# Spreading a row by stacked rounded products, and moving weight splits between VectorE's products

## The chip, the cores and the metric

The kernel runs on one core of one Trainium2 chip. The metric is the device time of one execution in microseconds; the time before is the median of three runs, 1167.11 us (1166.09 to 1169.34).

## What is computed

The model is two blocks over 256 tokens of width 1024. The change touches two mixers of the second block. The first is a linear attention with four heads, in which a running maximum over the tokens weighs each score:

```
dmat = where(tri, bcum[t] - bcum[s] + i[s], -inf)
m_t  = maximum(inter, max(dmat))
s    = einsum('td,sd->ts', q, k) * exp(dmat - m_t)
den  = w_inter * q.n + sum(s)
h    = num / maximum(abs(den), exp(-m_t))
```

The second is an eight-head softmax attention over the 256 tokens, the last attention of the model:

```
q = rope(rmsnorm(q)) ; k = rope(rmsnorm(k))
o[h] = softmax(mask(q[h] @ k[h].T) / sqrt(128)) @ v[h]
out = concat(o) @ w_o
```

Around them stand three feed-forward stages (up projection, a convolution of width 3, gate, down projection). All operands are fp32.

## The kernel before

**Weights.** All projections read one stream of weights, cut into slots of 128 x 1024 elements. SyncE loads a slot into a ring of eight, as TensorE gives slots back. TensorE multiplies in the rounded fp32 type, so each operand is split in two: ScalarE writes the rounded upper half of the slot (its split), then VectorE writes the rest in place (`split_one`, a subtraction over 128 x 1024, L1863). A projection then takes three rounded products for each block. TensorE waits for VectorE's half before the first block of each slot. ScalarE may write the upper half of a slot only when TensorE has begun the slot three earlier, since those halves have a ring of four.

**Order.** Each engine runs one list of instructions in program order. The places of the splits in VectorE's list are written out by hand, as `split_to(n)`: do all splits up to slot n. Any instruction of VectorE that stands ahead of a split delays it, and any split that stands ahead of a product delays the product.

**Linear heads.** VectorE forms rows of four partitions, one per head: a scan for the cumulated gates (`rowF`), the row `rowG`, a scan for the running maximum, and its sum with `rowF`. The last two fill `rowM2` (L2372 and L2373). Behind them stand the splits of slots 161 to 164 and 165 (`split_to(L0+4)`, L0 is 164). TensorE meanwhile runs the value projections lv (slots 156 to 163) and lo0 (164, 165). It then takes the heads one by one (`l_scores`, L1080): the product `mb` spreads a head's row over 128 partitions, by a 4 x 128 matrix of ones and zeros (`sel`) times the 4 x 512 row, in plain fp32; `sc` is the head's score product. VectorE adds the mask (`decay_in`), ScalarE takes the exponential, VectorE multiplies by the scores (`weighted`), TensorE makes the sum and the values (`l_values`: `dn`, `nm`) and the norm's sum (`hn`). Between them TensorE runs halves of the projections lo1 to lo3 (`gate_half`).

**Last attention.** TensorE projects bq, bk, bv. VectorE rotates q and k (`rope`), then multiplies each by its heads' inverse norms (`head_scaled`, four products over 128 x 512, for q and for k). On bk's and bv's slots the order of VectorE's list is: splits up to slot 263, q's four products, splits of 264 to 266, k's rotation (with 267 and 268 inside), k's four products, splits of 269 to 271. The slots 262 to 269 are bv's, 270 and later are those of the output projection bo. TensorE makes scores 0 and 1 ahead of the last two k-steps of bv10 and bv11 (slot 269); scores 2 need a bank that ScalarE frees by copying bv10. Then the heads turn in a ring: `a_max` (VectorE: mask and row extreme), `a_exp` (ScalarE: exponential with its sum), the scaling by the inverse sum (VectorE, L2534 to L2537), `turn` (TensorE: three transposes, L1168), a copy (ScalarE), `values` (TensorE), copies of the result (ScalarE), and the rest of its split (GpSimd). VectorE's order is a_max 0, a_max 1, scaling 0, a_max 2, scaling 1, a_max 3, scaling 2 and so on.

Of the kernel before, what the change touches and what calls it, by code (L numbers as in the profile page):

```python
# [21 lines left out]
ALU = mybir.AluOpType  # L22
# [3 lines left out]
P = 128  # L26
T = 256
# [41 lines left out]
def constants():  # L69

    c = np.zeros((P, NCON), np.float32)

    def put(name, a):
        at, k = CCOL[name]
        c[:a.shape[0], at:at + k] = a
    i = np.arange(P)
    s, t = i[:, None], i[None, :]
    same = (s // CH) == (t // CH)
    put("ident", np.eye(P))
    put("ones", np.ones((P, P)))  # L80
    put("bones", same * 1.0)
    strict, incl = same & (s < t), same & (s <= t)
    put("mask4", np.concatenate([strict * 1.0, incl * 1.0, strict * -1.0, incl * 1.0], 1))
    lev = []
    for m in (1, 2, 4, 8, 16, 32):

        off = (s // (2 * m) == t // (2 * m)) & ((s // m) % 2 == 1) & ((t // m) % 2 == 0)
        level = np.eye(P) - off
        lev.append(np.concatenate([level[:CH, :CH], level[CH:, CH:]], 0))
    put("lev", np.concatenate(lev, 1))  # L90
    put("idc", (s % CH == np.arange(CH)[None, :]) * 1.0)
    put("rev", (s >= t) * 1.0)
    z = np.zeros((P, P))
    put("negS", np.concatenate([(s >= t) * NEG, z, (s >= t) * NEG], 1))
    put("posI", np.concatenate([(s > t) * -NEG, z], 1))
    put("negC", np.concatenate([(t > s) * NEG, z, (t > s) * NEG], 1))
    half = 16
    inv = 500000.0 ** (-np.arange(0, 32, 2, dtype=np.float32) / np.float32(32))
    ang = np.arange(T, dtype=np.float32)[None, :] * inv.astype(np.float32)[:, None]
    cos, sin = np.ones((P, T)), np.zeros((P, T))  # L100
    cos[:half] = cos[half:2 * half] = np.cos(ang)
    sin[:half], sin[half:2 * half] = np.sin(ang), -np.sin(ang)
    put("cos", cos)
    put("sin", sin)
    put("scan", np.tile((np.arange(T) % CH != 0) * 1.0, (P, 1)))
    sel = np.zeros((4, 4 * P))
    for h in range(4):
        sel[h, h * P:(h + 1) * P] = 1.0
    put("sel", sel)
    put("one", np.ones((P, T)))  # L110
    put("eps", np.tile(np.array([[1e-6, 64e-5]]), (P, 1)))
    return c
# [32 lines left out]
SLOT_END = slot_ends()  # L145
# [35 lines left out]
def program(nc, ins, out):  # L181
    ctx = ExitStack()
    with ctx:
        sems = {}

        def sem(name):
            if name not in sems:
                sems[name] = ctx.enter_context(nc.semaphore(name))
            return sems[name]
# [55 lines left out]
        def view(kb, c, n, off=0):  # L245
            at = int(kb * KB) + off
            half = int(MID * KB)
            assert at >= half or at + c * n <= half
            v = arena[:, at:at + c * n] if at < half else arena2[:, at - half:at - half + c * n]
            return v.rearrange("p (c n) -> p c n", c=c) if c > 1 else v  # L250
# [11 lines left out]
        base = 78.5  # L262
# [76 lines left out]
        rowF = view(base + 25, 1, T)  # L339
        rowG = view(base + 26, 1, T)  # L340
        rowM2 = view(base + 27, 1, 2 * T)
        rowT = view(base + 29, 1, T)
        EM = view(base + 30, 2, T)
        ET = view(base + 32, 2, 384)
# [7 lines left out]
        ak = view(base + 8, KD, T)  # L352
        aq = view(base + 16, KD, T)
# [13 lines left out]
        def cst(name, rows=P):  # L367
            at, k = CCOL[name]
            if at >= NCON1:
                return con2[0:rows, at - NCON1:at - NCON1 + k]  # L370
            return con1[0:rows, at:at + k]
# [12 lines left out]
        def fr(ap):  # L384

            first = ap.tensor.name == arena.name
            row = int(MID * KB) if first else int((ARENA - MID) * KB)
            part_, at = ap.offset // row, ap.offset % row + (0 if first else int(MID * KB))
            for (a, b), place in zip(places, rounded):
                if a * KB <= at < b * KB:  # L390
                    w = int((b - a) * KB)
                    return bass.AP(tensor=place, offset=part_ * w + at - int(a * KB),
                                   ap=[[w, ap.ap[0][1]]] + [list(x) for x in ap.ap[1:]])
            raise AssertionError(at / KB)
# [12 lines left out]
        def rd(ap):  # L407

            return fr(ap).bitcast(F32)
# [68 lines left out]
        def _(pe):  # L478
            state = {"slot": 0, "blk": 0, "A": 0, "B": 0, "C": 0, "inc": False}

            def mm(o, l, r, start, stop, shared=False):
                ins_ = nc.tensor.matmul(o, l, r, start=start, stop=stop, skip_group_check=shared)  # L482
                if state["inc"]:
                    ins_.then_inc(sem("slots_used"), 1)
                    state["inc"] = False
                return ins_
# [38 lines left out]
            def close(ins_, name):  # L525
                ins_.then_inc(full(name)[0], 1)
# [226 lines left out]
            for u, name in enumerate(("mqn0", "mqn1", "mkn0", "mkn1")):  # L753
                o = open_(name)
# [95 lines left out]
            for i in range(0, 16, 2):  # L850
                t, c = i // 8, i % 8 // 2
                o = [open_(f"qd{i}"), open_(f"qd{i + 1}")]
# [227 lines left out]
            def l_scores(h):  # L1080
                o = open_(f"mb{h}")
                if h == 0:
                    ready(pe, "m_row")
                close(mm(o[:, :], cst("sel", 4)[:, h * P:(h + 1) * P], rowM2[0:4, :], True, True), f"mb{h}")
                o = open_(f"sc{h}")
                if h == 0:
                    pe.wait_ge(*freed("lk1"))
                mm(o[:, 0:T], lqk[:, 4 + h, 0:P], lqk[:, h, :], True, True)
                close(mm(o[:, T:T + P], lqk[:, 4 + h, P:T], lqk[:, h, P:T], True, True), f"sc{h}")
# [757 lines left out]
        def _(dve):  # L1847
            own = [0]

            def mark(ins_):  # L1850
                own[0] += 1
                ins_.then_inc(sem("dve_step"), 1)
# [4 lines left out]
            def step(ins_):  # L1857

                mark(ins_)
                settle()  # L1860
# [7 lines left out]
            def split_to(end):  # L1868
                while split[0] < min(end, nslots):
                    split_one(split[0], split[0] + 1)  # L1870
                    split[0] += 1
# [17 lines left out]
            def tt(o, a, b, op):  # L1889
                return V.tensor_tensor(o, a, b, op)  # L1890
# [451 lines left out]
            ffn(0, "r2", "n2", "x2", "l", "an")  # L2342

            dve.wait_ge(sem("ld_con"), 48)
            split_to(SLOT_END["lq0"] + 3)
            dve.wait_ge(*freed("r3"))
            step(V.reciprocal(rstd, rstd))
# [21 lines left out]
            step(V.tensor_tensor_scan(rowF[0:4, :], cst("one", 4), rowLF[0:4, :], 0.0, ALU.mult, ALU.add))  # L2369
            tt(rowG[0:4, :], rowG[0:4, :], rowF[0:4, :], ALU.subtract).then_inc(sem("g_row"), 1)  # L2370
            ready(dve, "g_row")
            step(V.tensor_tensor_scan(rowM2[0:4, 0:T], cst("one", 4), rowG[0:4, :], 0.0, ALU.mult, ALU.max))  # L2372
            tt(rowM2[0:4, T:2 * T], rowM2[0:4, 0:T], rowF[0:4, :], ALU.add).then_inc(sem("m_row"), 1)  # L2373

            def decay_in(h):
                o = take(f"mb{h}")
# [121 lines left out]
                    if u % 2:  # L2498
                        split_to(min(split[0] + 1, end))

            def head_scaled(x, dst, n0):

                settle()
                for u in range(4):
                    c = slice(2 * u, 2 * u + 2)
                    ready(dve, "a_inv", n0 + u + 1)
                    tt(dst[:, c, :], atm[x][:, c, :], asq[x][:, c, :], ALU.mult).then_inc(sem("a_rope"), 1)
            split_to(SLOT_END["bk1"] + 2)
            rope("q", aq, 0, SLOT_END["bk2"] + 2)
            split_to(SLOT_END["bk3"] + 2)  # L2510
            head_scaled("q", aq, 0)
            split_to(SLOT_END["bk3"] + 5)
            rope("k", ak, 4, SLOT_END["bk3"] + 7)
            head_scaled("k", ak, 4)
            split_to(SLOT_END["bv11"] + 2)

            def a_max(h):
                o = take(f"as{h}")
                if h >= 3:
                    dve.wait_ge(*full(f"at{h - 3}"))  # L2520
                for t in range(TT):
                    s = slice(t * P, 3 * P if t else P)
                    last = V.tensor_tensor_reduce(aP[:, h % 3, s], o[:, s], cst("negC")[:, s], -P ** -0.5, 3e38,  # L2523
                                                  ALU.add, ALU.min, small[:, 56 + 2 * h + t:57 + 2 * h + t])
                    if t == 0:
                        mark(last)
                    else:
                        release(last, f"as{h}")
            a_max(0)
            a_max(1)  # L2530
            for h in range(8):
                ready(dve, "a_e", 2 * h + 2)
                rs = small[:, 72 + 2 * h:74 + 2 * h]
                step(V.reciprocal(rs, rs))  # L2534
                p_ = aP[:, h % 3, :]
                step(V.tensor_scalar(p_[:, 0:P], p_[:, 0:P], rs[:, 0:1], None, ALU.mult))
                V.tensor_scalar(p_[:, P:3 * P], p_[:, P:3 * P], rs[:, 1:2], None, ALU.mult)\  # L2537
                    .then_inc(sem("a_p"), 1)
                if h < 6:
                    a_max(h + 2)  # L2540
            split_to(SLOT_END["bv11"] + 3)
# [90 lines left out]
```

## Time and profile before

| | value |
|---|---|
| median of three runs | 1167.11 us |
| the profiled execution | 1166.16 us, of which the span is 1164.4 us |
| TensorE busy | 1141.5 us, 98% of the span |
| VectorE busy | 936.8 us, 80% |
| ScalarE busy | 694.9 us, 60% |
| granted TensorE clock | 1.0 of full speed (2.4 GHz) throughout |

The page's chain of work is followed back from the last instruction. A piece of it that belongs to TensorE is time that only shorter or fewer products save; a piece of VectorE or ScalarE is time in which TensorE had to wait for them. Times in the timelines are microseconds from the span's start.

### The profile page before, as it was taken

The page shows a single profiled execution, that of the slowest core. Times are in us where ns is not written, and L with a number is a line of the kernel's source. Part 1 is how long each engine was busy: PE and PEld are TensorE (multiplying, and loading weights), DVE is VectorE, ACT ScalarE, POOL GpSimd, SP SyncE. Part 2 cuts the span into 40 slices and gives each one's busy share as a digit, 9 for nine tenths or more (in the row PEclk, how much of TensorE's full clock was granted, in tenths as well). Part 3 has the DMA queues.
Part 4 walks back from the last instruction along what each step waited for, and adds up shares of the span by engine and source line. Part 5 has one row for each costly group of instructions (what it writes and reads, how often), then busy time and mean ns, then how long its engine had stood idle before and what let it go on. Part 6 is the DMA issues. An engine that isn't in the chain of part 4 may idle for free.

```text
span 1164.4 us, 23202 instructions
## 1 busy us (share of the span) xinstructions
PE 1141.5 (98%) x9164; PEld 1052.7 (90%) x9164; DVE 936.8 (80%) x1369; ACT 694.9 (60%) x1075; POOL 332.0 (29%) x252
## 2 busy tenths in 40 slices
PE   9999999999999999999999999999999999999998
PEld 8988778878899999989888999998899789999987
DVE  5989774458878999866658799998679968999963
ACT  6787854346656666644557566665455666666642
POOL 2334111000013555311202235552128123555500
PEclk9999999999999999999999999999999999999999
DMA  8744211225556555554442455555554425555552
GB/s 311 238 151 140 97 37 40 86 98 199 188 189 203 184 186 186 176 189 176 157 156 93 151 192 182 182 182 182 196 178 155 145 86 181 181 183 182 181 186 86
DMA packets 55012, 188.95 MB, mean 162 GB/s; under 512 B 6144, under 2 KB 7296, under 8 KB 54784
## 3 DMA queue, kind: packets, MB, share of 16 engines
q1 hardware_dynamic: 53312, 182.48, 45.0%
q10 hardware_dynamic: 1600, 5.05, 1.3%
q8 instruction: 73, 1.20, 0.4%
q14 instruction: 27, 0.22, 0.1%
HBM read 186.46 MB, written 1.05 MB: 161 GB/s over the span
## 4 chain that ended last, share of the span: by engine, by line
PE 51%; DVE 36%; issue 6%; ACT 6%; DMA 1%; SPq 0%; ACTq 0%; DVEq 0%
PE psA L482 41%; DVE rounded L1890 18%; DVE arena L1893 13%; PE psB L482 9%; DVE arena L1890 3%; ACT rounded L1236 2%; ACT arena L1236 2%; ACT L1236 1%; DMA arena<-in_w 1%; DVE arena L2300 0%; DVE rounded L1893 0%; PE psB L792 0%; PE psB L1168 0%; DVE arena L2523 0%; PE psB L775 0%
## 5 line engine op out<-in xcount | busy, mean ns | idle before, releaser
L482 PE MATMUL psA<-rounded,rounded 128*128 128x256 f32 (+1 forms) x7236 | 1003.3, 300 | 11.0 <-DVE rounded L1890 10.0
L482 PEld LDWEIGHTS psA<-rounded,rounded 128*128 128x128 f32 x7236 | 940.0, 191 | 67.0 <-DVE rounded L1890 12.3
L1890 DVE TENSOR_TENSOR rounded<-arena,rounded 128x1024 fp32r<-128x1024 f32 (+2 forms) x364 | 475.5, 1338 | 61.3 <-ACT rounded L1236 58.7
L1236 ACT ACTIVATE rounded<-arena 128x1024 fp32r<-128x1024 f32 (+2 forms) x508 | 415.3, 858 | 168.8 <-DVE arena L2259 61.0
L1722 POOL TENSOR_TENSOR arena<-arena 128x256 f32<-128x256 f32 (+1 forms) x113 | 180.5, 1603 | 551.2 <-ACT arena L1236 201.1
L1236 ACT ACTIVATE arena<-arena 128x256 f32<-128x256 f32 (+8 forms) x313 | 163.3, 552 | 177.5 <-DVE arena L2324 109.4
L1893 DVE SCALAR_TENSOR_TENSOR arena<-arena 128x255 f32<-128x255 f32 (+4 forms) x338 | 190.6, 607 | 12.5 <-ACT arena L1236 9.9
L482 PE MATMUL psB<-arena 64*64 64x64 f32 (+9 forms) x1448 | 129.4, 281 | 4.4 <-issue 2.6
L482 PEld LDWEIGHTS psB<-arena 64*64 64x64 f32 (+4 forms) x1448 | 91.1, 152 | 31.5 <-issue 21.0
L1890 DVE TENSOR_TENSOR arena<-arena,psA 128x256 f32<-128x256 f32 (+1 forms) x101 | 45.5, 450 | 49.3 <-PE psA L482 39.0
L1807 POOL TENSOR_TENSOR rounded<-arena,rounded 128x256 fp32r<-128x256 f32 x63 | 71.9, 1142 | 34.0 <-ACT rounded L1236 34.0
L1236 ACT ACTIVATE arena<-psA 128x256 f32<-128x256 f32 (+2 forms) x75 | 35.3, 477 | 52.3 <-PE psA L482 51.7
L1890 DVE TENSOR_TENSOR arena<-arena 128x256 f32<-128x256 f32 (+5 forms) x85 | 55.2, 667 | 10.2 <-ACT arena L1236 8.7
L1890 DVE TENSOR_TENSOR arena<-psA,arena 128x512 f32<-128x512 f32 x79 | 54.0, 686 | 5.2 <-PE psA L482 2.4
L1236 ACT ACTIVATE arena<-psB 128x512 f32<-128x512 f32 (+4 forms) x61 | 28.4, 496 | 42.9 <-PE psB L482 40.1
L1236 ACT ACT_TABLE_LOAD x41 | 52.6, 1283 | 2.0 <-PEq L2626 1.2
L1890 DVE TENSOR_TENSOR arena<-psB,arena 128x512 f32<-128x512 f32 (+5 forms) x55 | 29.3, 561 | 28.6 <-PE psB L482 27.9
L1893 DVE SCALAR_TENSOR_TENSOR rounded<-arena,rounded 128x256 fp32r<-128x256 f32 x48 | 32.3, 687 | 18.2 <-ACT rounded L1236 18.2
L1728 POOL TENSOR_TENSOR rounded<-arena,rounded 128x256 fp32r<-128x256 f32 x24 | 21.7, 929 | 36.2 <-ACT rounded L1236 36.2
L1236 ACT ACTIVATE arena<-psB,arena 128x256 f32<-128x256 f32 (+1 forms) x45 | 23.6, 564 | 12.3 <-PE psB L482 7.1
L1737 POOL TENSOR_TENSOR arena<-arena 128x512 f32<-128x512 f32 x15 | 20.4, 1359 | 1.2
L1783 POOL TENSOR_TENSOR arena<-arena 64x256 f32<-64x256 f32 x8 | 5.9, 739 | 39.6 <-DVE arena L1890 39.3
(75 smaller groups left out, 183.7 us busy)
## 6 DMA issues: line engine op xcount, KB each, us to landing
arena<-in_w SPq DMA_DIRECT2D x343, 512.0 KB, 3.5
arena<-in_mem ACTq DMA_DIRECT2D x2, 512.0 KB, 7.3
arena<-in_x ACTq DMA_DIRECT2D x1, 1024.0 KB, 5.2
out<-arena SPq DMA_DIRECT2D x8, 128.0 KB, 3.3
arena<-in_con ACTq DMA_DIRECT2D x1, 992.0 KB, 5.9
arena<-in_con ACTq DMA_DIRECT2D x1, 960.0 KB, 7.4
arena<-in_w SPq DMA_DIRECT2D x2, 256.0 KB, 3.3
arena<-in_x SPq DMA_DIRECT2D x2, 256.0 KB, 5.0
```

The lines of the kernel that those rows point to most:

```text
L482: ins_ = nc.tensor.matmul(o, l, r, start=start, stop=stop, skip_group_check=shared)
L1236: return nc.scalar.activation(o, i, f, **kw)
L1722: return nc.gpsimd.tensor_tensor(o, a, b, ALU.mult)
L1728: nc.gpsimd.tensor_tensor(fr(x[:, c, :]), x[:, c, :], rd(upper_[:, c, :]), ALU.subtract)\
L1737: nc.gpsimd.tensor_tensor(dst[:, 0:2, :], dst[:, 0:2, :], dst[:, c, :], ALU.add)\
L1783: nc.gpsimd.tensor_tensor(LT[h, 4 * g:4 * g + 4, :], quadA[h, 4 * g:4 * g + 4, h], bc(cst("idc")[h], 4), ALU.add).then_inc(sem("LT"), 1)
L1807: nc.gpsimd.tensor_tensor(lr_, gv[:, j % 2, :], hi, ALU.subtract)\
L1890: return V.tensor_tensor(o, a, b, op)
L1893: return V.scalar_tensor_tensor(out=o, in0=a, scalar=s, in1=b, op0=op0, op1=op1)
```

## The change

It has two parts.

**The row's spread.** The constant `sel` gets 36 rows, with its four rows of ones a second time at 32 to 35, and VectorE rounds it once, ahead of the linear mixer's first splits. The scan and the sum now fill a plain row `rowM`. Its rounded upper part goes to partitions 0 to 3 of `rowM2` and the rest to 32 to 35; partitions 0 to 31 are set to zero first. The product `mb` is one of the rounded type over these 36 partitions. Per head it replaces the plain fp32 product over 4.

**The last attention.** In `head_scaled` a split follows the first and the third product. For q these are slots 264 and 265, with 266 behind the fourth product. For k they are 269 and 270; slot 271 is split after a_max 0 and a_max 1. VectorE's order at the heads becomes a_max 0, a_max 1, split 271, scaling 0, scaling 1, a_max 2, a_max 3, scaling 2, a_max 4, scaling 3, and so on.

```diff
-    sel = np.zeros((4, 4 * P))
+    sel = np.zeros((36, 4 * P))
     for h in range(4):
-        sel[h, h * P:(h + 1) * P] = 1.0
+        sel[h, h * P:(h + 1) * P] = sel[32 + h, h * P:(h + 1) * P] = 1.0
...
+        rowM = view(base + 58, 1, 2 * T)
...
-                close(mm(o[:, :], cst("sel", 4)[:, h * P:(h + 1) * P], rowM2[0:4, :], True, True), f"mb{h}")
+                close(mm(o[:, :], fr(cst("sel", 36))[:, h * P:(h + 1) * P], fr(rowM2)[0:36, :], True, True), f"mb{h}")
...
             dve.wait_ge(sem("ld_con"), 48)
+            mark(V.tensor_copy(fr(cst("sel", 36)), cst("sel", 36)))
             split_to(SLOT_END["lq0"] + 3)
...
-            step(V.tensor_tensor_scan(rowM2[0:4, 0:T], cst("one", 4), rowG[0:4, :], 0.0, ALU.mult, ALU.max))
-            tt(rowM2[0:4, T:2 * T], rowM2[0:4, 0:T], rowF[0:4, :], ALU.add).then_inc(sem("m_row"), 1)
+            mark(V.memset(rd(rowM2)[0:32, :], 0.0))
+            step(V.tensor_tensor_scan(rowM[0:4, 0:T], cst("one", 4), rowG[0:4, :], 0.0, ALU.mult, ALU.max))
+            step(tt(rowM[0:4, T:2 * T], rowM[0:4, 0:T], rowF[0:4, :], ALU.add))
+            step(V.tensor_copy(fr(rowM2)[0:4, :], rowM[0:4, :]))
+            tt(fr(rowM2)[32:36, :], rowM[0:4, :], rd(rowM2)[0:4, :], ALU.subtract).then_inc(sem("m_row"), 1)
...
-            def head_scaled(x, dst, n0):
+            def head_scaled(x, dst, n0, end):
...
                     tt(dst[:, c, :], atm[x][:, c, :], asq[x][:, c, :], ALU.mult).then_inc(sem("a_rope"), 1)
+                    if u % 2 == 0:
+                        split_to(min(split[0] + 1, end))
...
-            head_scaled("q", aq, 0)
+            head_scaled("q", aq, 0, SLOT_END["bk3"] + 5)
             split_to(SLOT_END["bk3"] + 5)
             rope("k", ak, 4, SLOT_END["bk3"] + 7)
-            head_scaled("k", ak, 4)
-            split_to(SLOT_END["bv11"] + 2)
+            head_scaled("k", ak, 4, SLOT_END["bv11"] + 1)
+            split_to(SLOT_END["bv11"] + 1)
...
             a_max(0)
             a_max(1)
-            for h in range(8):
+            split_to(SLOT_END["bv11"] + 2)
+            a_part(0)
+            a_part(1)
+            a_max(2)
+            a_max(3)
+            for h in range(2, 8):
+                a_part(h)
                 if h < 6:
                     a_max(h + 2)
```

`a_part(h)` holds the scaling of a head that stood in the loop's body before (L2534 to L2537).

## Rows read from the trace of the kernel before

**Rows 1.** The page, parts 1 and 4: busy time and the chain's shares.
```profile
PE 1141.5 (98%) x9164; PEld 1052.7 (90%) x9164; DVE 936.8 (80%) x1369; ACT 694.9 (60%) x1075; POOL 332.0 (29%) x252
...
PE 51%; DVE 36%; issue 6%; ACT 6%; DMA 1%; SPq 0%; ACTq 0%; DVEq 0%
```

**Rows 2.** Chain of work, 550 to 680: start us, us, what.
```profile
571.73 27.73 PE psA L482 x144
...
604.68 3.87 PE psB L482 x18
...
611.42 4.73 PE psB L482 x22
...
625.75 2.83 PE psB L482 x16
```

**Rows 3.** TensorE's groups by form, 571.6 to 594.6: count, busy us, mean ns.
```profile
L482 PE MATMUL psA<-rounded,rounded 128*128 128x512 f32 x96 | 22.1, 390 | 0.0
```

**Rows 4.** Timeline, 600 to 615: start us, us, engine, what, idle before and its releaser.
```profile
600.47 1.28 ACT L1236 ACT_TABLE_LOAD   x1
...
603.98 1.23 DVE L1890 TENSOR_TENSOR rounded<-arena,rounded 128x1024 fp32r<-128x1024 f32 x1 [2.23 <-ACT rounded L1236]
...
605.13 0.55 DVE L1890 TENSOR_TENSOR arena<-arena,psB 128x384 f32<-128x384 f32 x1
605.66 2.69 PEld L482 LDWEIGHTS psB<-arena 128*128 128x128 f32 x16 [0.76 <-issue]
...
612.50 0.75 DVE L1890 TENSOR_TENSOR arena<-psB,arena 128x256 f32<-128x256 f32 x2 [1.29 <-PE psB L482]
```

**Rows 5.** Timeline, 582 to 590: the row's end and what follows.
```profile
583.29 4.85 DVE L1890 TENSOR_TENSOR rounded<-arena,rounded 128x1024 fp32r<-128x1024 f32 x4
...
585.82 1.07 ACT L1236 ACTIVATE rounded<-arena 128x1024 fp32r<-128x1024 f32 x1 [0.45 <-PE psA L482]
```

**Rows 6.** VectorE's groups by form, whole span: count, busy us, mean ns, idle before.
```profile
L1890 DVE TENSOR_TENSOR rounded<-arena,rounded 128x512 fp32r<-128x512 f32 x9 | 6.0, 689 | 4.1 <-ACT rounded L1236 3.8
...
L2191 DVE COPY arena<-arena 64x512 f32<-64x512 f32 x1 | 0.4, 408 | 0.0
...
L1907 DVE MEMSET arena<- 128x256 f32 x1 | 0.3, 272 | 0.9 <-PEq L2626 0.9
```

**Rows 7.** Timeline, 549 to 552: VectorE ahead of the linear mixer.
```profile
549.87 1.22 DVE L1890 TENSOR_TENSOR rounded<-arena,rounded 128x1024 fp32r<-128x1024 f32 x1 [0.48 <-ACT rounded L1236]
```

**Rows 8.** Timeline, 904 to 924: q's products, the splits, k's products.
```profile
904.57 3.30 POOL L1722 TENSOR_TENSOR arena<-arena 128x512 f32<-128x512 f32 x2 [5.04 <-ACT arena L1236]
905.18 4.44 DVE L1890 TENSOR_TENSOR arena<-arena 128x512 f32<-128x512 f32 x4
909.54 3.48 DVE L1890 TENSOR_TENSOR rounded<-arena,rounded 128x1024 fp32r<-128x1024 f32 x3
...
910.81 5.76 PE L482 MATMUL psA<-rounded,rounded 128*128 128x512 f32 x24 [1.93 <-DVE rounded L1890]
...
923.72 2.50 DVE L1890 TENSOR_TENSOR arena<-arena 128x512 f32<-128x512 f32 x4 [0.91 <-ACT arena L1236]
```

**Rows 9.** Timeline, 929 to 948: the heads of the last attention.
```profile
929.54 0.28 DVE L2523 CUSTOM_DVE_ANT_0 arena<-psA,arena 128x128 f32<-128x128 f32 x1
...
932.63 0.92 PE L482 MATMUL psA<-arena 128*128 128x128 f32 x4 [0.38 <-ACT arena L1236]
...
933.59 0.29 DVE L2523 CUSTOM_DVE_ANT_0 arena<-psA,arena 128x128 f32<-128x128 f32 x1 [1.47 <-PE psA L482]
...
935.17 0.52 PE L1168 MATMUL psB<-arena 128*128 128x128 f32 x3 [0.63 <-DVE arena L2537]
...
940.00 0.39 ACT L1236 ACTIVATE arena<-arena 128x128 f32<-128x128 f32 x1
...
941.80 0.40 ACT L1236 ACTIVATE arena<-arena 128x128 f32<-128x128 f32 x1
...
943.88 0.39 ACT L1236 ACTIVATE arena<-arena 128x128 f32<-128x128 f32 x1
```

More of the change, by code:

```diff
@@ L2528, in a_max, with a_part @@
                         release(last, f"as{h}")
-            a_max(0)
-            a_max(1)
-            for h in range(8):
+            def a_part(h):
                 ready(dve, "a_e", 2 * h + 2)
@@ L2538, in _ @@
                     .then_inc(sem("a_p"), 1)
+            a_max(0)
+            a_max(1)
+            split_to(SLOT_END["bv11"] + 2)
[5 more added lines that the diff above has]
+                a_part(h)
                 if h < 6:
```

## The prediction, made before the changed kernel was seen

> **What bounds the kernel now.** I read the page first: TensorE is busy 98% of the span and holds 51% of the chain, VectorE 36% [rows 1]. An average says nothing of the two stages that change, so I read the chain of each, then its timeline.
>
> In the linear mixer the chain is TensorE alone from 571.73 us on, through all four heads. The reader is to see blocks of rounded projections, and between them one block per head on the other bank set [rows 2]. There a shorter product shortens the path, until another engine's result is late. The closest is VectorE's `weighted` 0 [rows 4].
>
> In the last attention three things take turns. TensorE stands 1.93 us before slot 264, until VectorE has split it [rows 8]. From 910.81 to 932.2 it is busy again. From 932.63 to 947.8 the heads go round, and all three engines are nearly full [rows 9].
>
> **Spread, what TensorE saves.** What a `mb` costs now comes out of the blocks of the chain. The block of 16 instructions (hn, dn, nm) has 3328 columns by instruction, each plain product being two: 2.83 us, or 0.85 ns a column [rows 2]. By that price sc, dn and nm of a head (768, 768 and 1536 columns) take 2.61 us, and the block of 18 leaves 3.87 - 2.61 = 1.26 us for `mb`; with hn (0.87) the block of 22 leaves 1.25. Its 1024 columns are worth 0.87 us; the other 0.4 us is a pause around a product of four rows, also seen as 0.76 us in which no weight load begins behind it [rows 4]. A rounded product of 512 columns costs 22.1 / 96 = 0.23 us [rows 3]. No row shows a product of 36 rows. From one side the pause goes (`mb` 0.23, 1.03 saved), from the other it grows by as much again (1.03, 0.23 saved). I take it as staying: 0.63, or 0.63 saved per head, since every row of a short product has it.
>
> The Trainium skill (TensorEngine Tiling (Array Packing), Key Properties) says that a change of tiling mode drains TensorE. The pause in the trace agrees with that, and 36 rows would still be a smaller tile than 128, so by it the drain stays, which speaks against the full gain. Read as a drain that goes with the small tile, the rule gives 0.63 a head; without it 1.03 would hold.
>
> **Spread, where the saving meets a wait.** The plain sum is 4 x 0.63 = 2.5 us. Head 0's sum `dn` also needs `weighted` 0, which ends at 605.13 + 0.55 = 605.68. That chain hangs on ScalarE's table load at 600.47, behind the small `gcol` product that stands ahead of `mb`, and on the split at 603.98, so it doesn't move [rows 4]. `dn` 0 begins now near 604.68 + 1.26 + 0.65 = 606.6, and cannot begin before 605.73. So after heads 0 and 1 the gain is 0.85, not 1.26. Heads 2 and 3 add 0.63 each: VectorE idles 1.29 us before `decay_in` 2 [rows 4], as much as it is then to come forward. Together 2.1 us, which pass on to hn 1 and so to the chain's next pieces in ScalarE and VectorE. Bounds: 0.23 a head gives 0.9; 1.03 a head gives 0.85 + 2 x 1.03 = 2.9.
>
> **Spread, what VectorE pays.** Four things are new ahead of the split of slot 161. The memset over 32 x 512 has 128 x 256 at 0.27 as nearest row, so 0.54 for twice the columns (0.27 to 0.69). The rounding copy of 4 x 512 has 64 x 512 at 0.41 (to 0.69). The subtraction has 128 x 512 at 0.69 [rows 6]. Two more waits for the own result take 0.1 or a little less. Sum 1.7 us, 1.4 to 2.2. Behind them in VectorE's list stand the splits of 161 to 165, and TensorE waits for those. Slot 161 is split by 583.29 + 1.21 = 584.50 now. TensorE begins it near 585.4: ScalarE was released at 585.80 by the end of its first product, which takes 0.39 [rows 3, 5]. So the margin is 0.9, and TensorE will stand 1.7 - 0.9 = 0.8 us (0.5 to 1.3). Slot 162 follows at 1.2 us in VectorE and 2.8 in TensorE, so nothing adds up. Rounding `sel` (0.4 to 0.7) comes ahead of the split at 549.87, before which VectorE idles 0.48 [rows 7]. It is taken at nothing; what is over the idle time, up to 0.2, would move this stage's later splits, and all 0.7 of it if that idle weren't there.
>
> Net for the spread: 2.1 - 0.8 = **1.3 us** (from 0.9 - 1.3 = -0.4 to 2.9 - 0.5 = 2.4).
>
> **Attention, q's side.** TensorE is at slot 264 at 908.88 and gets it at 910.81. After the change the split follows q's first product: 905.18 + 1.19 = 906.37, plus 1.2 to 1.9 for a split beside GpSimd, which works until 907.87. So it is there by 907.6 to 908.3, and the 1.93 us go [rows 8]. Slots 265 and 266 end at about 910.5 and 912.3 and are needed at 911.8 and 917.5. The products that move back have no hurry, as scores begin at 928. TensorE then has no gap until slot 269 is done, because from 910.81 on it had none.
>
> **Attention, k's side.** ScalarE's inverse norms follow TensorE's sums and come 1.2 us or more earlier, so k's products begin when VectorE is through with its rotation, about 0.9 earlier: it idled 0.91 there [rows 8]. VectorE's list from 905.18 to there is otherwise the same work. In it, slot 269 is ready long before 927.2; slot 270 must wait for ScalarE's upper half, which comes behind two copies at 925.3, in time for the split at 925.9. With one split fewer ahead, a_max 0 starts near 927.7 instead of 929.54 [rows 9]. Split 271 (1.16) then fills the time in which ScalarE takes the first exponentials; scaling 0 would follow near 930, with or without it. Scores 2 hang on the copy of bv10, that is on TensorE's last products (1.9 earlier) and on a_exp 1 (1.9 earlier): 930.75 instead of 932.63.
>
> **Attention, the ring.** Before, VectorE waited 1.47 us for scores 2 [rows 9] while scaling 1 was ready to go behind it; TensorE then stood 0.63 for scaling 1 at 935.17. Now scaling 1 fills that wait, turn 1 comes near 932.4, and the second score pair is not held up. Then ScalarE sets the pace: its work for a head takes 1.8 us where it doesn't wait (940.00 to 941.80 between two exponentials) [rows 9]. Scores 2 at 930.75 give a_max 2 at 931.7 and the exponential of head 2 at 932.5. That of head 3 follows 1.4 later (no result to copy yet), those of 4 to 7 at 1.8 to 1.9 each, so head 7's begins at 932.5 + 1.4 + 4 x 1.86 = 941.35. Before, it was at 943.88 [rows 9]. So the order alone brings about 0.6, not the sum of the waits. Attention in all: 943.88 - 941.35 = 2.5, of which I keep **2.4 us** for GpSimd's contention with VectorE in the ring. Bounds: only the stall before 264 less a collision of one split's excess, 1.3; all of it with the 1.9 standing waits in the ring, 3.4.
>
> Behind the ring the bo projection and the last feed-forward stage follow by dependences, with TensorE the longest in front; nothing there is late because the ring ends earlier (ScalarE and VectorE stand idle before bo's second slot).
>
> **Sum.** 1.3 + 2.4 = 3.7 us. The profiled execution takes 1166.16 us, 1.76 of it outside the span, and that stays: 1162.5. It lies 0.95 under the median of the runs; on the median it is **1163.4 us**.
>
> **The rivals.**
> - *The spread brings nothing.* The row work is at its dear end and the pause grows at 36 rows, so the stall before slot 161 eats the saving (-0.4 to 0.5); attention keeps 2.4: 1164.7. For it: no row shows either operation. Against: the rounded product alone must take 0.64 us off each of four products.
> - *The stall moves.* The 1.93 us before slot 264 go, but the same VectorE work then stands before a later slot or before a_max, and the ring is paced by ScalarE as before: attention 1.3, with the spread 1.3, 1164.5 to 1165.5. For it: VectorE is full from 905 to 929. Against: it idles 0.91 before k's products [rows 8] and 1.47 before a_max 2 [rows 9].
> - *More than I count.* The pause goes and the ring gives all waits back: 2.4 + 3.2 = 5.6, 1161.5.
> - *Slower than before.* The place is the row chain before slot 161. Beyond 0.9 us each added microsecond there is one of TensorE's. It decides when the new work exceeds 0.9 + 2.1 + 2.4 = 5.4 us, that is when small operations that write rounded rows at partition 32 take 1.7 us each, not 0.4 to 0.7; at 2.4 each (7.2 us) the time is 1169. Only VectorE's reciprocals take that long.
> - *It doesn't do what it says.* If a product of 36 rows isn't one pass but two as before, it costs 0.87 and the pause: no saving, the stall stays, 2.4 - 0.8 = 1.6: 1165.5.
>
> **How the numbers follow.** What a measurement here can tell from no change is about 0.3%, 3.5 us, so the border is at 1163.6. Chances: forecast 0.50 (its own width 0.9 us either way, so a little over half of it beyond the border), spread brings nothing 0.13, stall moves 0.16, more than I count 0.12, slower 0.04, two passes 0.05. Faster by over 0.3%: 0.28 + 0.12 and a bit of the next two, 0.43. Slower by over 0.3%: 0.04. The range leaves out the slow case and the ends of the outer two: 1160.8 to 1165.8.
>
> **What would show it.** Right: `mb` as one rounded instruction a head, the blocks with it 0.6 us shorter; TensorE idle 0.5 to 1.3 before slot 161, near 585.4; no idle before slot 264; `dn` 0 still right behind `weighted` 0; a_max 0 near 927 less what the spread gave; head 7's exponential 2.4 earlier against the stage's start. Wrong: a stall before slot 161 above 1.5 us, blocks shorter by less than 0.3, or a new idle time of TensorE between 911 and 932. The last would undo the attention part first.

## The result

The changed kernel takes 1160.87 us (median of five runs, 1159.94 to 1162.40) against 1167.11 us (five runs, 1165.47 to 1169.34). The ratio is 0.9945, with a 95% interval from 0.9931 to 0.9960: faster by 6.2 us, 0.55%. The forecast was 3.7 us faster, 1163.4 us. The range (1160.8 to 1165.8) just holds the time, but the forecast gave "within 0.3%" the larger chance, 0.53 against 0.43 for faster, and that was wrong.

The profiled execution of the changed kernel has a span of 1159.0 us (1160.88 us with what lies around it), 5.4 us less than before. Where do the 5.4 us lie? Five pieces can be cut by rows that both kernels have. The first fence is the kernel before, the second the changed one. The rows are ScalarE's first operation on the gate rows (4x256), a pair of ScalarE operations at the end of the linear mixer, GpSimd's last pair of products for k, and the last rounded copy of a head's result. Columns are start, duration, engine, line and what.

```profile
span 1164.4 us, 23202 instructions
...
573.49 0.42 ACT L1236 ACTIVATE arena<-arena 4x256 f32<-4x256 f32 x1 [6.96 <-DVE arena L2363]
...
640.80 0.73 ACT L1236 ACTIVATE arena<-arena 128x256 f32<-128x256 f32 x2
...
948.08 0.39 ACT L1236 ACTIVATE rounded<-psB 128x256 fp32r<-128x256 f32 x1 [0.29 <-PE psB L482]
```

```profile
span 1159.0 us, 23197 instructions
...
570.33 0.42 ACT L1237 ACTIVATE arena<-arena 4x256 f32<-4x256 f32 x1 [6.97 <-DVE arena L2365]
...
636.88 0.73 ACT L1237 ACTIVATE arena<-arena 128x256 f32<-128x256 f32 x2
...
900.68 3.30 POOL L1723 TENSOR_TENSOR arena<-arena 128x512 f32<-128x512 f32 x2 [5.06 <-ACT arena L1237]
...
941.64 0.39 ACT L1237 ACTIVATE rounded<-psB 128x256 fp32r<-128x256 f32 x1 [0.47 <-PE psB L483]
```

GpSimd's row of before is the first of [rows 8], at 904.57. The differences, in us:

| piece | before | after | gain |
|---|---|---|---|
| start to the gate rows | 573.49 | 570.33 | 3.16 |
| linear mixer | 67.31 | 66.55 | 0.76 |
| second feed-forward stage, bq, bk | 263.77 | 263.80 | -0.03 |
| last attention, to its last head | 43.51 | 40.96 | 2.55 |
| bo and the last feed-forward stage | 216.3 | 217.4 | -1.0 |

So the two changed stages gain 3.3 us, near the forecast's 3.7. The rest lies in pieces that the change doesn't touch, above all ahead of it. Whether that comes with the change was the first question for the experiments.

**The linear mixer after.** These are TensorE's waits from 572 to 640, by releaser: us in total, times, longest.

```profile
PE psA L483 <- DVE rounded L1891: 2.1, 3, 0.9
PE psB L483 <- DVE arena L1891: 0.4, 1, 0.4
```

Two of the three in the first line are old: the one of 0.92 us stood at 637.75 before, and one of 0.42 at 643.46, outside the window. Two waits are really new, one in each line (0.76 and 0.39), and the timeline shows both, with the row work ahead of the first.

```profile
579.20 0.48 DVE L2374 MEMSET rounded<- 32x512 f32 x1 [0.16 <-DVE arena L1891]
...
580.70 0.41 DVE L2377 CAST rounded<-arena 4x512 fp32r<-4x512 f32 x1
581.15 5.34 DVE L1891 TENSOR_TENSOR rounded<-arena,rounded 4x512 fp32r<-4x512 f32 x5
583.14 14.01 PEld L483 LDWEIGHTS psA<-rounded,rounded 128*128 128x128 f32 x84 [1.18 <-DVE rounded L1891]
583.14 14.21 PE L483 MATMUL psA<-rounded,rounded 128*128 128x512 f32 x84 [0.76 <-DVE rounded L1891]
...
602.99 0.55 DVE L1891 TENSOR_TENSOR arena<-arena,psB 128x384 f32<-128x384 f32 x1
...
603.69 2.20 PE L483 MATMUL psB<-arena 128*128 128x256 f32 x12 [0.39 <-DVE arena L1891]
...
608.69 0.49 PE L483 MATMUL psB<-rounded,rounded 36*128 36x512 f32 x1
```

TensorE stands before slot 161 (583.14), and `dn` 0 (603.69) stands right behind `weighted` 0 (602.99), both as forecast. The product is one rounded instruction. The chain has the head blocks, to be held against the blocks of 18 and 22 instructions in [rows 2] (start, us, what):

```profile
608.76 4.10 PE psB L483 x21
...
615.73 3.24 PE psB L483 x17
...
621.83 2.83 PE psB L483 x16
```

4.73 has become 4.10 and 3.87 has become 3.24: 0.63 each. The block without a spread is 2.83 as before.

**The last attention after.** Its timeline, where the reader is to look for the wait before slot 264 (it had been 1.93), the start of a_max 0, scores 2, turn 1, and the exponential of head 7:

```profile
901.30 1.53 DVE L1891 TENSOR_TENSOR arena<-arena 128x512 f32<-128x512 f32 x1
902.75 2.31 DVE L1891 TENSOR_TENSOR rounded<-arena,rounded 128x1024 fp32r<-128x1024 f32 x1
...
905.12 5.32 PEld L483 LDWEIGHTS psA<-rounded,rounded 128*128 128x128 f32 x24 [0.55 <-DVE rounded L1891]
...
923.67 0.29 DVE L2530 CUSTOM_DVE_ANT_0 arena<-psA,arena 128x128 f32<-128x128 f32 x1
...
926.75 0.92 PE L483 MATMUL psA<-arena 128*128 128x128 f32 x4 [0.21 <-ACT arena L1237]
...
928.49 0.49 PE L1169 MATMUL psB<-arena 128*128 128x128 f32 x3
...
937.16 0.40 ACT L1237 ACTIVATE arena<-arena 128x128 f32<-128x128 f32 x1
```

The split beside GpSimd took 2.31 us and is just late: TensorE's weight loads still wait 0.55 (2.35 before). All times in this stage are told from the start of GpSimd's row, 904.57 before and 900.68 after. TensorE's next block, the sums of k's norms, starts at 10.02 us (11.84 before, so 1.82 of the 1.93 us arrive there), a_max 0 at 22.99 (24.97), scores 2 at 26.07 (28.06), turn 1 at 27.81 (30.60) and head 7's exponential at 36.48 (39.31). That exponential is 2.83 us earlier; the last head's result is 2.55 earlier. Between the two, TensorE's last four products stand 0.24 us for ScalarE.

### The profile page after: what moved, and what is told of

Read it like the earlier page. It is cut to its first block, busy times and chain, and to the rows that moved or that the text cites. A ratio compares the mean times of both kernels' runs of the same rounds, so it can differ in the third digit from the quotient of the medians.

```text
span 1159.0 us, 23197 instructions
## 1 busy us (share of the span) xinstructions
PE 1138.7 (98%) x9160; PEld 1053.0 (91%) x9160; DVE 938.3 (81%) x1373; ACT 694.1 (60%) x1075; POOL 332.0 (29%) x252
## 4 chain that ended last, share of the span: by engine, by line
PE 48%; DVE 38%; issue 7%; ACT 6%; DMA 1%; SPq 0%; DVEq 0%; ACTq 0%
PE psA L483 39%; DVE rounded L1891 18%; DVE arena L1894 14%; PE psB L483 8%; DVE arena L1891 3%; ACT rounded L1237 3%; ACT arena L1237 2%; ACT L1237 1%; DMA arena<-in_w 1%; DVE arena L2301 0%; DVE rounded L1894 0%; PE psB L793 0%; DVE arena L2495 0%; PE psB L1169 0%; PE psB L776 0%
## 5 line engine op out<-in xcount | busy, mean ns | idle before, releaser
L483 PE MATMUL psB<-arena 64*64 64x64 f32 (+9 forms) x1440 | 125.7, 279 | 5.1 <-issue 2.8
```

## The experiments

Theory A: the parts are worth what their stages show, and the rest scatters from execution to execution, with either kernel. Theory B: the untouched pieces became faster by the change. Four kernels ran side by side.

**e1, the kernel before as its own rival.** No edit.

> The kernel before, unchanged, timed as if it were a change. Theory A (the parts are worth 0.9 and 2.5 us, as their own stages show, and the other 3 us of the trace lie in stages that both kernels share and differ from one execution to the next): its median within 2 us of the kernel before, and its trace shifted by up to 3 us against the first trace of before in stages ahead of 550 us. Theory B (executions repeat to 0.5 us and the 3 us come with the change): shift below 0.5 us everywhere.

Measured: 1167.49 us against 1167.21, ratio 0.9997 (0.9986 to 1.0007). Its row of the gates lies at 573.87, only 0.38 us from the first profile's 573.49, which by itself would suit theory B. Its tail behind the last head is 217.3 us, where the first profile of the same program has 216.3; B's 0.5 us everywhere doesn't hold there.

**e2, the changed kernel again.** No edit.

> The changed kernel once more. Theory A: 3 to 5 us faster than before instead of 6.2. Theory B: 6 us again, and the stages ahead of 550 us again 3 us earlier than those of before.

Measured: 1164.06 against 1167.21, 3.15 us by the medians, ratio 0.9964 (0.9949 to 0.9978). The row at which the linear mixer begins, in the trace of e1 and then of e2:

```profile
573.87 0.42 ACT L1236 ACTIVATE arena<-arena 4x256 f32<-4x256 f32 x1 [6.97 <-DVE arena L2363]
```

```profile
573.09 0.42 ACT L1237 ACTIVATE arena<-arena 4x256 f32<-4x256 f32 x1 [6.96 <-DVE arena L2365]
```

573.09, where the first profile of the same program had 570.33. Against B: the 3.2 us ahead of the change don't come with it each time. The two changed stages repeat, with 66.52 and 40.96 us.

**e3, the attention part alone.** The edit is the second half of the diff.

> Only the attention part: splits between the products, scaling 0 and 1 ahead of the third extreme. Both theories: no wait of TensorE before slot 264, and the stage from q's products to the last exponential 2.4 to 2.6 us shorter. Theory A: 2.5 us faster in all. Theory B: more than 4 us.

Measured: 1164.29 us, ratio 0.9974 (0.9963 to 0.9984), 3.0 us (2.9 by the medians). The stage takes 945.99 - 905.07 = 40.92 us, 2.59 less than before.

**e4, the spread alone.** The edit is the first half of the diff.

> Only the spread by stacked rounded products. Both theories: TensorE waits 0.8 us before slot 161, head blocks 0.63 us shorter each, net 0.9 us in the stage. Theory A: 0.9 us faster in all, not told from nothing. Theory B: more than 2 us.

Measured: 1166.38 us, ratio 0.9989 (0.9979 to 0.9999), 1.3 us by the ratio, 0.8 by the medians. In its trace the attention is as before (948.61 - 905.12 = 43.49) and the linear mixer takes 66.53 us, 0.78 less. The four together speak for A: the parts bring what their stages show, and B's 3 us ahead of them are ruled out. A smaller share there, up to about one, is not (see what stays open).

The next four kernels ran once each, so their whole times mean nothing at this size, and each is read by the length of its own stage. That can be trusted: over the traces of this case with the same code in the stage, the linear mixer scatters by 0.03 us and the attention by 0.07. The stages are cut as follows: the linear mixer from ScalarE's 4x256 row to the last block of four plain products in the chain (635.18 - 573.49 = 61.69 us before, 631.27 - 570.33 = 60.94 after), the attention from GpSimd's row to the last head (43.51 and 40.96).

**e5, the split of slot 161 ahead of the row work.**

```diff
+            split_to(L0 - 2)
             mark(V.memset(rd(rowM2)[0:32, :], 0.0))
```

> The changed kernel, with the split of slot 161 ahead of the new row work instead of behind it. If TensorE's 0.76 us before slot 161 are the row work's (forecast's step), that wait is gone, slot 162 (needed 2.8 us later) is in time, and the stage from the first value product to the gate projections' end is 0.7 to 0.8 us shorter. Rival (the wait is ScalarE's, whose upper half of the slot is late): the wait stays.

Measured: TensorE waits nowhere from 572 to 600. The stage is 633.94 - 574.08 = 59.86, so 1.08 shorter than with the late split, not 0.76. The delay is thus larger than the idle time that TensorE's row shows. The rows say why: in the stream a product begins every 0.23 us but its row lasts 0.39 [rows 3], so the row's idle time starts 0.16 us after the next product could have begun; and behind the wait the second product follows the first by 0.34 instead of 0.23. That makes 0.76 + 0.16 + 0.11 = 1.03 of the 1.08.

**e6, a longer row.**

```diff
-            step(V.tensor_copy(fr(rowM2)[0:4, :], rowM[0:4, :]))
+            for _ in range(5):
+                step(V.tensor_copy(fr(rowM2)[0:4, :], rowM[0:4, :]))
```

> The changed kernel with the rounding copy of the row made five times, 4 x 0.44 = 1.8 us more ahead of the split of 161. Forecast's rule (each microsecond beyond the margin is one of TensorE's): the wait before slot 161 grows from 0.76 to 2.5 us and the stage by 1.8 us. Rival (the wait is absorbed before the heads begin, as ScalarE's table load sets head 0): the stage grows by less than 0.9 us.

Its wait before slot 161:

```profile
586.33 3.93 PE L483 MATMUL psA<-rounded,rounded 128*128 128x512 f32 x16 [2.55 <-DVE rounded L1891]
```

The wait grew by 1.79 and the stage to 634.43 - 571.72 = 62.71, by 1.77 us. So the rule holds one for one, as the forecast had it: once the margin is gone, added VectorE work ahead of that split is TensorE time.

**e7, splits between q's products alone.**

```diff
-            def head_scaled(x, dst, n0):
+            def head_scaled(x, dst, n0, end=0):
...
                     tt(dst[:, c, :], atm[x][:, c, :], asq[x][:, c, :], ALU.mult).then_inc(sem("a_rope"), 1)
+                    if u % 2 == 0:
+                        split_to(min(split[0] + 1, end))
...
-            head_scaled("q", aq, 0)
+            head_scaled("q", aq, 0, SLOT_END["bk3"] + 5)
```

> The kernel before, with splits between q's products alone. Forecast: the wait of 1.93 us before slot 264 goes, and 1.9 us of it arrive at the heads' end. Rival (the stall moves): it returns before a later slot or before the first extreme, and less than 1.2 us arrive.

The stage is 946.17 - 903.54 = 42.63, 0.88 shorter, so the forecast of 1.9 fails and the rival holds: the stall has moved. The three splits behind k's products still stand ahead of a_max 0 (24.15 us from GpSimd's row, 24.97 before, 22.99 with the whole change), the exponentials follow late, and TensorE waits for ScalarE's copy of bv10 before scores 2 (it was 0.38):

```profile
927.69 0.28 DVE L2525 CUSTOM_DVE_ANT_0 arena<-psA,arena 128x128 f32<-128x128 f32 x1
...
930.13 1.05 ACT L1236 ACTIVATE arena<-psA 128x512 f32<-128x512 f32 x2
...
930.75 0.92 PE L482 MATMUL psA<-arena 128*128 128x128 f32 x4 [1.35 <-ACT arena L1236]
```

**e8, the ring's order alone.** The kernel before, with scaling 0 and 1 put ahead of a_max 2 and 3; the splits stay where they were. The edit repeats the scaling's lines in place.

```diff
             a_max(1)
             for h in range(8):
+                if h == 1:
+                    continue
+                if h == 0:
+                    for g in range(2):
+                        ready(dve, "a_e", 2 * g + 2)
...
+                    a_max(2)
+                    a_max(3)
+                    continue
                 ready(dve, "a_e", 2 * h + 2)
```

> The kernel before, with scaling 0 and 1 ahead of the third extreme alone. Forecast: the order alone brings 0.6 us at the last exponential, as ScalarE sets the pace. Rivals: nothing (0.0 to 0.2), or TensorE's waits before the turns (1.9 us in all) come back in full.

The stage is 947.43 - 904.53 = 42.90, 0.61 shorter. At the last exponential, for which the 0.6 was forecast, it is 0.88: 942.96 - 904.53 = 38.43 against 39.31.

```profile
942.96 0.40 ACT L1236 ACTIVATE arena<-arena 128x128 f32<-128x128 f32 x1
```

So of the 2.55 us q's splits alone bring 0.88 and the order 0.61. The remaining 1.06 is left for the splits between k's products, the later split 271 and whatever the parts do only together; none of that was run by itself.

The last three kernels ask what the 0.4 us around the spread product is, try a better version, and time the changed kernel a third time. The diffs of e9 and e10 are against e5.

**e9, four rows, still rounded.** It leaves out the lower parts of the row values, so it is a probe of the pause and no version to keep.

```diff
-                close(mm(o[:, :], fr(cst("sel", 36))[:, h * P:(h + 1) * P], fr(rowM2)[0:36, :], True, True), f"mb{h}")
+                close(mm(o[:, :], fr(cst("sel", 4))[:, h * P:(h + 1) * P], fr(rowM2)[0:4, :], True, True), f"mb{h}")
```

> As the early split, but the rounded product takes only the four upper rows, so the rest of each row value (its lower part) is left out of the sum. If the pause of 0.4 us around the product goes with a tile of few rows, it stays, as with 36 rows: block of 17 instructions at 3.24 us. If it goes with the plain type, it is gone in both and nothing differs either.

**e10, all 128 rows.**

```diff
-                close(mm(o[:, :], fr(cst("sel", 36))[:, h * P:(h + 1) * P], fr(rowM2)[0:36, :], True, True), f"mb{h}")
+                close(mm(o[:, :], fr(cst("sel"))[:, h * P:(h + 1) * P], fr(rowM2)[:, :], True, True), f"mb{h}")
...
-            mark(V.tensor_copy(fr(cst("sel", 36)), cst("sel", 36)))
+            mark(V.tensor_copy(fr(cst("sel")), cst("sel")))
...
-            mark(V.memset(rd(rowM2)[0:32, :], 0.0))
+            mark(V.memset(rd(rowM2), 0.0))
```

> As the early split, but the rounded product runs over all 128 rows, the others being zero. If the pause belongs to the change between a small tile and the full one, it goes: the blocks of heads 2 and 3 fall from 3.24 to 2.84 us, 0.8 us in all, while heads 0 and 1 stay bound to the first weighted scores. Together with the early split 1.5 us faster than the changed kernel. Rival (the pause belongs to the change between rounded and plain products): the blocks stay at 3.2 us, and the gain is the early split's 0.76 alone.

The same two blocks of the chain, of e9 and then of e10:

```profile
607.50 4.10 PE psB L483 x21
...
614.47 3.23 PE psB L483 x17
```

```profile
608.85 3.72 PE psB L483 x21
...
615.43 2.85 PE psB L483 x17
```

With 4 or 36 rows the block is the same; with 128 it is 0.38 shorter. So the pause belongs to a product of few rows among products of 128, and the rounded type alone doesn't take it away. A plain product over 128 rows wasn't run. In e10 the wait of `dn` 0 is 0.95 instead of 0.39:

```profile
603.78 2.20 PE L483 MATMUL psB<-arena 128*128 128x256 f32 x12 [0.95 <-DVE arena L1891]
```

So heads 0 and 1 gave nothing more, and the stage is 630.60 - 571.49 = 59.11, 0.75 shorter than in e5. Times: e9 1161.65 us, ratio 0.9955 (0.9939 to 0.9971); e10 1160.64 us, ratio 0.9945 (0.9926 to 0.9964), both against 1166.97.

**e11, the changed kernel a third time.**

> The changed kernel a third time, as the neighbour of the two variants. If its first time (6.2 us faster) was the upper end of what executions scatter, it is again 3.5 to 4.5 us faster than before. If two loads of one program differ lastingly, it could be at 6 again.

Measured: 1162.49 us, ratio 0.9967 (0.9952 to 0.9983), 4.5 us by the medians. Its neighbour e10 is 1.85 us faster by the medians, and the stages say 1.08 + 0.75 = 1.83. e10 beats both kernels.

## Why the prediction was right or wrong

**Sum of the stages.** Forecast 3.7, measured 3.3 in the stages. The paths and waits were the forecast ones. Two terms of the spread had the wrong size, what the heads save and what the row work costs.

- *The saving per head.* 0.63 forecast, 0.63 measured in the blocks of 21 and 17. The choice that the pause stays was right. The Trainium skill (TensorEngine Tiling (Array Packing), Key Properties) says that a change of tiling mode drains TensorE. The traces of e9 and e10 agree with it: the block loses 0.38 us when the spread's product has 128 rows like its neighbours, and nothing between 36 rows and 4.
- *Where it meets a wait.* `dn` 0 behind `weighted` 0, as said. Heads in all: the stage shrank by 1.83 in e5, where the forecast had 2.1. Heads 2 and 3 gave their 0.63 each, so heads 0 and 1 gave 0.57 and not 0.85. I put the start of `dn` 0 at 606.6 by sums of block prices; the trace of before has its first weight load at 606.31, only 0.58 behind the bound of 605.73, and that is the difference.
- *The row work.* 1.7 us forecast. VectorE's time from the start of `rowG`'s subtraction to the split of 161 rose from 583.29 - 581.79 = 1.50 to 581.86 - 578.62 = 3.24, by 1.74. The margin was taken as 0.9. By e5 the cost is 1.08, so the margin was 0.66; this is the mis-sized term. I had worked out when slot 161's first product begins (585.4; it began at 585.39), but what waits for the split is its weight load, and that stands 0.22 us earlier in the trace of before, 0.67 behind the split's end at 584.50:

```profile
585.17 0.19 PEld L482 LDWEIGHTS psA<-rounded,rounded 128*128 128x128 f32 x1
```

- *Net of the spread.* Saved 2.1 forecast, 1.83 measured; cost 0.8 forecast, 1.08 measured. Net 1.3 forecast, 0.76 measured.
- *Rounding `sel`.* Taken as 0.4 to 0.7 at no cost. It took 1.51 us beside GpSimd, and still cost nothing that shows: from the second load of `x` to the gate rows e4, which has it, takes 307.03 us, before and e1 307.07 and 307.04.
- *The stall before 264.* It went as said, all but 0.11. The first product took 1.45 us up to the split's start (1.19 forecast) and the split 2.31 (1.2 to 1.9 forecast), both beside GpSimd, so the split was there 4.38 us after GpSimd's start and not within 3.7.
- *The stall moves.* This rival is true of q's part by itself: only 0.88 of 1.82 us arrive (e7). The forecast was right to count k's splits with it, but e7's expectation called the 1.9 us q's. With the whole change they arrive at a_max 0 (1.98 earlier), so about half of them need more than q's part; which of the other parts it is was not run.
- *The ring.* 0.6 forecast for the last exponential, 0.88 measured there and 0.61 at the last head's result (e8). ScalarE paces it, as said: after the change the exponentials of heads 3 to 7 follow each other by 1.78 to 2.12 us (1.86 forecast). Attention: 2.4 forecast for head 7's exponential, 2.83 measured there, 2.55 at the last head's result. That 2.55 lies so near 2.4 is in part luck: more was gained up to the exponential than said, and 0.28 of it was lost behind it, which the forecast had at nothing.
- *The slower rival.* e6 confirms its mechanism, one for one, and the small operations ahead of the split took 0.41 to 0.68 us, so it was never near its point.

**The whole time.** The step that failed is the last one, from the sum to the chances. It had a sum of 3.7 us, just past the border of 3.5 us (0.3%), and gave "within 0.3%" 0.53, since it let the outcome scatter by "its own width 0.9 us either way" and put what an execution does outside the two stages at nothing. The runs showed that this is the larger part. Three timings of the one changed program gave 6.2, 3.15 and 4.5 us by the medians, ratios 0.9945, 0.9964 and 0.9967. In the first, the changed stages hold 3.3 of the profile's 5.4 us, and 3.2 lie ahead of them, less 1.0 behind. In other profiles of the same two programs these pieces come out otherwise: 573.09 against 570.33 for the lead, 217.3 against 216.3 for the tail. That the range just holds 1160.87 is therefore no proof of its reasons: the low end stood for a pause that goes and waits that all come back, and neither happened. Over all three timings, 22 runs, the median is 1162.4 against 1167.15 for 53 runs of before: about 4.7 us, all three intervals clear of no change. That is 0.40%, past 0.3%, on the side of the border where the forecast's own sum lay too.

**What stays open.** The stages show 3.3 us, the timings together more: e11 shows 1.2 over its stages, e3 0.3, e9 0.9 and e10 1.2, while e2 (3.15), e4 (0.8) and e1 show nothing. The traces have a candidate ahead of both stages. From the second load of `x` (near 266 us) to the gate rows, where the rounding of `sel` is all that the change adds, all five profiles without the spread take 306.97 to 307.07 us. Of the eight with it, three take 307.0 (e2, e4, e5), three 306.0 (e6, e10, e11) and two 305.1 (the first one and e9). So the shorter lengths came only with the spread, but not each time, and the one changed program shows all three of them. The two rows in its first profile (305.12) and in e2 (306.99):

```profile
265.21 0.33 ACTq L1518 DMA_DIRECT2D arena<-in_x  x1
...
570.33 0.42 ACT L1237 ACTIVATE arena<-arena 4x256 f32<-4x256 f32 x1 [6.97 <-DVE arena L2365]
```

```profile
266.10 0.33 ACTq L1518 DMA_DIRECT2D arena<-in_x  x1
...
573.09 0.42 ACT L1237 ACTIVATE arena<-arena 4x256 f32<-4x256 f32 x1 [6.96 <-DVE arena L2365]
```

The mean of the eight is 0.9 us below the five. With one profile per timing that is no proof, and why such a piece changes its length is not known; a part of theory B, about one microsecond, is therefore not excluded.

## What to carry to other kernels

Count small row operations by what stands behind them in the same engine's list: here 1.74 us on four partitions cost 1.08 us of TensorE, and one split moved ahead of them gave it back. Measure the margin of a wait at the weight load, not at the product. When a stall is removed by reordering, look for the next gate of the same list; q's splits alone returned half. A product of few rows among full ones can be worth padding with zero rows; here that gave 0.38 us for each of two heads, where nothing else was waited for. And when the forecast gain is as small as the scatter of the median, give that scatter its share of the chances.

## What the runs showed of the hardware that was not expected

- A single rounded product with 4 or 36 rows between products of 128 rows cost 0.38 us more than one padded to 128 rows (blocks of 3.23 and 3.24 us against 2.85). The plain one of four rows in the kernel before has about the same pause, 0.4 us, by the prices of its block.
- Stages with the same code take one of two lengths. From the end of the linear mixer to GpSimd's row it is 263.7 to 263.8 us in six of the thirteen profiles (before, e1, the first of the changed kernel, e7, e9, e10) and 264.7 to 264.8 in the other seven, and the one changed program shows both (e2 and e11 have the longer). The tail behind the last head is 216.3 us in two (before, e4) and 217.2 to 217.4 in eleven. The rows of e11, which is the changed kernel again, 902.24 - 637.49 = 264.75:

```profile
637.49 0.73 ACT L1237 ACTIVATE arena<-arena 128x256 f32<-128x256 f32 x2
...
902.24 3.29 POOL L1723 TENSOR_TENSOR arena<-arena 128x512 f32<-128x512 f32 x2 [4.46 <-ACT arena L1237]
```

- The granted clock fell to its half (1.2 GHz) for a part of the stretch from 261 to 266 us in some executions of one program and not in others: its mean there is 0.66 in e1 (TensorE busy 4.66 of the 5 us ahead of it) and 1.00 in the first profile of before (busy 4.22 of 5). It lies ahead of the changed stages, and no stage length above holds it.
- Where TensorE waits for VectorE, the idle time in its own row (0.76) can be less than the delay (1.08, by e5), since the rows of products in a stream overlap. The weight loads' row (1.18) bounded it from above.
- An operation of VectorE beside one of GpSimd took up to about twice its time: in the changed kernel's first profile the split of 128 x 1024 took 2.31 us at 902.75, with GpSimd at work until 903.98, and 1.22 at 906.19 without it.
